# A residual stream kept feature by feature, with the norm's token factor multiplied into the accumulators of the next stage

## The reference

```python
def rmsnorm(x, g):
    return x * rsqrt(mean(x * x, axis=-1) + EPS) * g      # one factor per token, one gain per feature

def hybrid_layer(x, ...):                                  # first block
    h = rmsnorm(x, norm_g)
    aq, ak, av, az, bqk, bv, bi, bf, bo, bz, ga, gb = split(h @ w_in)
    q, k = rope(rmsnorm(heads(aq))), rope(rmsnorm(heads(ak)))
    oa = rmsnorm(diff_attention(q, k, av, lam)) * silu(az)   # 8 heads of 2 x 64, values of 128
    qk = silu(causal_conv(bqk))                              # 8 mLSTM heads
    hb = sigmoid(bo) * rmsnorm(mlstm(qk, bv, bi, bf)) * silu(bz)
    u = sigmoid(ga) * (oa @ w_out_a) + sigmoid(gb) * (hb @ w_out_b)
    return x + u @ w_o

# second block, one layer
h = rmsnorm(x, g_mix)
q_r, k_r, v_r, g_r, q_s, k_s, v_s, gate_a, gate_b = split(h @ w_in_2)
ret = group_norm(retention(rotary(q_r), rotary(k_r), v_r)) * silu(g_r)
sb = stick_breaking(q_s, k_s, v_s)
x = x + (sigmoid(gate_a) * (ret @ p_ret) + sigmoid(gate_b) * (sb @ p_sb)) @ w_out
x = x + square(relu(rmsnorm(x, g_mlp) @ w_up)) @ w_down
# after the last layer
return rmsnorm(x, g_final)
```

## Time and profile before

| | |
|---|---|
| median of three runs | 3214.42 us (3212.61 to 3216.8) |
| the profiled execution | 3216.47 us, span 3214.7 us |
| TensorE busy | 3179.6 us (99%) |
| GpSimd busy | 2072.9 us (64%) |
| VectorE busy | 1391.6 us (43%) |
| ScalarE busy | 843.1 us (26%) |
| moved by DMA | 298.58 MB, 93 GB/s in the mean |
| mean granted clock of TensorE | 0.999 |

### The profile page before, as it was taken

The page is one execution under the profiler, slowest core; times in us unless marked ns, Lnnn a source line. Parts: engine busy times, 40 slices in busy tenths (PEclk is TensorE's granted clock), DMA queues, the critical chain, the costliest instruction groups (busy, mean ns, idle before and its releaser), DMA issues.

```text
span 3214.7 us, 49199 instructions
## 1 busy us (share of the span) xinstructions
PE 3179.6 (99%) x15732; PEld 2676.8 (83%) x15732; DVE 1391.6 (43%) x2224; ACT 843.1 (26%) x1831; POOL 2072.9 (64%) x2052
## 2 busy tenths in 40 slices
PE   7999999999999999999999999999999999999999
PEld 6888888888888888888888888888888888888887
DVE  6777651237776531256663113111366652231121
ACT  5555340025554430032221012011122220021021
POOL 5556657765556567766666776666666657766665
PEclk9999999999999999999999999999999999999999
DMA  3222222232222222322222222223322222222222
GB/s 123 91 88 83 98 82 94 98 103 80 90 85 89 95 85 97 104 94 89 82 88 85 95 101 92 93 98 103 101 85 85 85 72 98 98 96 94 98 98 98
DMA packets 89615, 298.58 MB, mean 93 GB/s; under 512 B 12576, under 2 KB 13472, under 8 KB 89520
## 3 DMA queue, kind: packets, MB, share of 16 engines
q1 hardware_dynamic: 74592, 271.61, 25.3%
q10 hardware_dynamic: 14928, 25.67, 2.6%
HBM read 282.52 MB, written 2.13 MB: 89 GB/s over the span
## 4 chain that ended last, share of the span: by engine, by line
PE 95%; DVE 1%; DMA 1%; ACT 1%; POOL 1%; issue 0%; ACTq 0%; SPq 0%; POOLq 0%; DVEq 0%
PE bank L575 29%; PE bank L577 29%; PE bank L576 29%; PE bank L680 2%; PE bank L741 1%; PE bank L717 1%; PE bank L804 1%; PE bank L730 1%; PE bank L837 1%; POOL w_lo L559 0%; PE bank L786 0%; PE bank L675 0%; PE bank L693 0%; PE bank L821 0%; PE bank L822 0%
## 5 line engine op out<-in xcount | busy, mean ns | idle before, releaser
L559 POOL TENSOR_TENSOR w_lo<-raw,w_hi 128x512 fp32r<-128x512 f32 x1024 | 1385.4, 1353 | 85.4
L556 POOL TENSOR_SCALAR w_hi<-raw 128x512 fp32r<-128x512 f32 x1024 | 704.8, 688 | 1033.9 <-DMA raw<-in_w_in 699.3
L575 PE MATMUL bank<-h_lo,w_hi 128*128 128x512 f32 (+1 forms) x2912 | 1126.6, 387 | 5.9 <-POOL w_lo L559 4.8
L577 PE MATMUL bank<-h_hi,w_hi 128*128 128x512 f32 (+1 forms) x2912 | 1115.2, 383 | 0.0
L576 PE MATMUL bank<-h_hi,w_lo 128*128 128x512 f32 (+1 forms) x2912 | 1114.0, 383 | 0.0
L575 PEld LDWEIGHTS bank<-h_lo,w_hi 128*128 128x128 f32 x2912 | 548.4, 188 | 110.1 <-POOL w_lo L559 6.0
L577 PEld LDWEIGHTS bank<-h_hi,w_hi 128*128 128x128 f32 x2912 | 548.2, 188 | 108.5
L576 PEld LDWEIGHTS bank<-h_hi,w_lo 128*128 128x128 f32 x2912 | 548.8, 188 | 102.7
L1533 DVE TENSOR_TENSOR x<-x,bank 128x512 f32<-128x512 f32 x64 | 44.0, 687 | 391.4 <-PE bank L577 391.1
L575 PE MATMUL bank<-w_lo,up_hi 128*128 128x512 f32 x512 | 199.5, 390 | 0.0
L577 PE MATMUL bank<-w_hi,up_hi 128*128 128x512 f32 x512 | 199.2, 389 | 0.0
(11 more groups left out here) (291 smaller groups left out, 4254.1 us busy)
## 6 DMA issues: line engine op xcount, KB each, us to landing
raw<-in_w_in SPq DMA_DIRECT2D x288, 512.0 KB, 3.3
raw<-in_w_up SPq DMA_DIRECT2D x64, 512.0 KB, 3.3
raw<-in_w_down SPq DMA_DIRECT2D x64, 512.0 KB, 3.3
raw<-in_w_out_a SPq DMA_DIRECT2D x16, 512.0 KB, 3.3
raw<-in_w_out_b SPq DMA_DIRECT2D x16, 512.0 KB, 3.2
raw<-in_w_o SPq DMA_DIRECT2D x16, 512.0 KB, 3.3
raw<-in_p_ret SPq DMA_DIRECT2D x16, 512.0 KB, 3.3
raw<-in_p_sb SPq DMA_DIRECT2D x16, 512.0 KB, 3.2
```

The lines of the kernel that those rows point to most:

```text
L556: nc.gpsimd.tensor_scalar(m.w_hi[:, slot, w], m.raw[:, slot, w], 1.0, 0.0, ALU.mult, ALU.add).then_inc(s["w_step"], 1)
L559: nc.gpsimd.tensor_tensor(m.w_lo[:, slot, w], m.raw[:, slot, w], m.w_hi[:, slot, w].bitcast(F32), ALU.subtract).then_inc(s["split"], 1)
L575: nc.tensor.matmul(dst, hi, rhs_lo, start=first, stop=False, **more)
L577: return nc.tensor.matmul(dst, hi, rhs_hi, start=False, stop=last, **more)
```

## The change

`x` is kept feature-major, eight tiles of 128 features by 512 tokens, like every other activation. The host turns input and output. The projections become ordinary panels: `gemm` with the weights stationary, one bank each, 24 matmuls (48 for the down projection, over two panels). So the transposes, the half-width panels and the held panels go.

The norm's gain is one number a feature, now a column: `h = x * g` is split without waiting for the root. The token factor `r = rsqrt(mean(x^2) + eps)` is the same for all features, so it commutes with the matmul, and is multiplied in afterwards. The squares are summed over the eight tiles in `ssq`; one plain fp32 matmul with a 128 x 128 matrix of ones sums over the partitions and leaves the sum in all of them; two ScalarE operations make `r_b`, 128 x 512. VectorE multiplies the accumulator of a panel in place by `r_b` (`scaled`) before anyone reads it. The readers wait for the semaphore `scaled` in place of `used`. Not multiplied are the retention's queries and keys (there the cosine and sine tables are multiplied by `r_b` once a layer, and so loaded again each layer) and the up panels, where one operation takes max(accumulator, 0) times `r_b`. That makes 272 multiplied accumulators: 80 in a layer of the first block (32 in the head loop and last head, 32 in the pairs, 16 in the merge), 56 in one of the second.

On TensorE, at the start of a stage after a norm:

```diff
-            def first_panels():
...
-                early, late = slice(0, 2 * P), slice(2 * P, S)
-                turn_block(2)
...
-                half(0, early)
-                turn_block(3)
...
-                half(1, early)
...
+            def first_panel():
+
+                gemm(m.h_hi, m.h_lo, "h_ready", at.at("norm", times=KT))
                 at.add("norm")
...
+            def mean_square():
+
+                misc_bank()
+                pe.wait_ge(s["ssq_ready"], at.at("norm"))
+                nc.tensor.matmul(misc[:], m.ones[:], m.ssq[:], start=True, stop=True).then_inc(s["ms_done"], 1)
...
-                first_panels()
+                first_panel()
+                mean_square()
+                h_gemm()
                 pe.wait_ge(s["masks_ready"], 6)
                 group_sum(1, 0)
                 h_gemm()
                 group_sum(0, 0)
+                gate_rows(range(0, 6))
                 value_turns(0)
-                gate_rows()
+                gate_rows(range(6, KT))
```

With `ready`, `gemm` waits ahead of each of the eight tiles for that tile's low part. On ScalarE:

```diff
+            def norm():
+                for n in range(KT):
+                    act.wait_ge(s["x_done"], at.at("norm", times=KT) + (n + 1))
...
+                    activation(m.h_hi[:, n], m.x[:, n], ACT.Copy, scale=m.g_col[:, n:n + 1]).then_inc(s["h_hi_ready"], 1)
+                    if n > 1:
+                        act.wait_ge(s["ssq_added"], at.at("norm", times=KT) + n)
+                    activation((m.sq if n else m.ssq)[:], m.x[:, n], ACT.Square).then_inc(s["xsq_ready"], 1)
                 at.add("norm")
...
+            def root_row():
+                act.wait_ge(s["ms_done"], at.at("norm"))
+                own(activation(m.r_b[:], misc[:], ACT.Ln, bias=m.col[:, 2:3], scale=1.0 / D))
+                act.sem_inc(s["misc_free"], 1)
+                activation(m.r_b[:], m.r_b[:], ACT.Exp, scale=-0.5).then_inc(s["r_ready"], 1)
```

On VectorE, the multiplication, the norm and the head loop:

```diff
+            def scaled(read_here=False):
+
+                c = panel_done()
+                tt(acc[c][:], acc[c][:], m.r_b[:], ALU.mult).then_inc(s["scaled"], at.add("scaled"))
...
+            def residual_add(n, panels):
+                at.add("panel", panels - 1)
+                c = panel_done()
+                own(tt(m.x[:, n], m.x[:, n], acc[c][:], ALU.add))
+                dve.sem_inc(acc_free[c], 1)
+
+            def h_low(n):
+                dve.wait_ge(s["h_hi_ready"], at.at("norm", times=KT) + (n + 1))
+                stt(m.h_lo[:, n], m.x[:, n], m.g_col[:, n:n + 1], m.h_hi[:, n].bitcast(F32), ALU.mult,
+                    ALU.subtract).then_inc(s["h_ready"], 1)
+
+            def add_and_norm(panels):
+                for n in range(KT):
+                    residual_add(n, panels)
+                    dve.sem_inc(s["x_done"], 1)
+                    h_low(n)
+                    dve.wait_ge(s["xsq_ready"], at.at("norm", times=KT) + (n + 1))
+                    if n:
+                        own(tt(m.ssq[:], m.ssq[:], m.sq[:], ALU.add))
+                    dve.sem_inc(s["ssq_added"], 1)
+                dve.sem_inc(s["ssq_ready"], 1)
...
-                with at.loop(A_HEADS - 1, panel=4, acc=4, a=1, own=DVE_A) as i:
+                with at.loop(A_HEADS - 1, panel=4, acc=4, scaled=4, a=1, own=DVE_A) as i:
+                    c = scaled()
                     weights()
-                    cosines(0, 1, 1)
-                    rotate_qk(0, 1, 1)
-                    cosines(1, 1, 2)
+                    cosines(0, 1, 1, c)
+                    c = scaled()
+                    rotated(0, 1)
+                    queries_split()
+                    cosines(1, 1, 2, c)
                     key_squares_low(1)
-                    rotate_qk(1, 1, 2)
-                    take_panel()
+                    rotated(1, 1)
+                    scaled()
+                    keys_split(1, 2)
                     head_normalised()
-                    head_gate()
+                    c = scaled()
                     masked(1, 1)
+                    head_gate(c)
+                    other_maxima(1)
                     head_branch(i)
```

`masked` now takes the first of the four maxima, `other_maxima` the rest. At the end `y = x * g * r_b` is one operation a tile, after `r_b`, and goes out in eight stores of 256 KB:

```diff
+            dve.wait_ge(s["r_ready"], at.at("norm"))
+            for n in range(KT):
+                stt(m.y[:, n], m.x[:, n], m.g_col[:, n:n + 1], m.r_b[:], ALU.mult, ALU.mult).then_inc(s["y_ready"], 1)
```

592 lines of the change are left out of this document (261 added, 331 removed).

## The result

The changed kernel takes 3266.88 us (3265.97 to 3269.1, 4 runs), the kernel before beside it 3213.78 us: ratio 1.0165, 95% interval 1.0147 to 1.0182. It is slower by 53 us, where I forecast 12, with 3249 as the upper end. The profiled execution took 3267.22 us, its span 3265.4.

A forecast was written before the change was run, and what follows sets the result against it. TensorE, busy 3179.6 of 3214.7 us, was taken as the bound. Norms -26, start 0, end +5.5, head loop +18, last heads +10, second block +3, pairs +2: +12.5 on 3214.4 gives 3227, stated as 3226; range 3198 to 3249.

The forecast's parts named there:

- The head loop, +18 for the turns: First block's head loop: late V copy makes TensorE wait, 1.3 us a turn, fourteen turns, +18 us (0 to 36).
- The clock, put at nothing in the sum: TensorE at half clock behind waits: no term in the forecast's sum; 1.4 us lost behind a 1.9 us wait before.
- rival 3: Waits of 2.2 us in the head loop, likewise at last heads, lower the clock: 3247 us; chance 0.15, including slowest multiplication.
- The start, 0: Start to first scores: mean square waits 4 us, first scores about where they were; 0 us (-3 to +3).
- The norms, -26: Five norms between stages: transposes and waits go, 5 us each; scores' waits behind norms give 1 to 2 more; -26.
- The last heads, +10: Last head of a layer: V's multiplication behind gate rows, `o_sb` wait 3.7 us, about +5 a layer, +10 (4 to 14).
- The multiplication, 0.69: VectorE's in-place multiplication of 272 accumulators: 0.69 us each (0.51 to 1.65), covered in merges, up and down panels.
- The pairs of heads, +2: Pairs of heads: only the first of a layer waits; +2 us on the eight pairs (0 to 5).
- The end, +5.5: Kernel's end: 13.7 us from the last add to the span's end, 6.4 before; +5.5 us (4.5 to 7).
- The second block, +3: Second block's turns: key's low part has 0.33 us cover against 0.7 more, 0.4 a turn, 8 turns, +3 us.
- The rule on SBUF's ports: VectorE with at most one SBUF input, outside two-port modes, doesn't contend with GpSimd; with two it does. No sum term.

The follow-up runs named there:

- the second experiment: The changed kernel with ScalarE's logarithm and root of the keys' squares put ahead of V's copy in the head loop: 3245.96 us, ratio 1.0094.
- the kernel that it was made from: The changed kernel with V's multiplication put ahead of the keys' rotation on VectorE in the head loop: 3223.01 us, ratio 1.0027.

## Why the prediction was wrong

The direction was right, and so was the place where most of it is lost; the size was a quarter. The two profiled executions differ by 50.7 us, where the sum had 12.5. Of the 38 us between them 27 are the turns of the head loop (45 for 18), a good half of that the clock; 6.6 are the start. By its own steps:

- **The head loop, +18 for the turns.** This is the step that failed. It had 1.2 us of wait at the value turns. It followed V's multiplication to V's copy, and stopped there: it took the copy as the only thing for which the turns wait. They also wait for the bank that ScalarE's logarithm empties, behind the copy. The copy was 0.95 us late, and the logarithm's 0.25 + 0.69 us behind it make that the 1.95 to 2.0 measured; the second experiment put the logarithm ahead and found 1.2.
- **The clock, put at nothing in the sum.** The prediction left it to rival 3, with a chance of 0.15 and 3247 us; the terms of that rival's sum (31, 14 and 8) don't say which is the clock's. The waits came to 1.95 and the clock to 8 x 1.64 = 13. So rival 3's mechanism is what happened, 20 us above its time: 25.7 of waits at the value turns, 13 of half clock behind them, 6.0 for `o_sb`, 2.7 for the keys' squares, some 3 by which the turns grew beyond their waits (31.80 less 29.63 is 2.17, for a wait of 1.95), and 1.7 of half clock behind the second layer's first scores make up the 51.4 us that the two head loops' rows of the table show. Because the wait had been taken at 1.2, this case got too small a chance.
- **The start, 0.** It failed too: +6.6. The prediction followed the chain to the mean square (4.9 us of wait for the 4 forecast) and `r_b`, and not what stands in VectorE's queue behind the sum of squares: lambdas, a split of the gate weights and conversions, 9.6 us from 26.44 to 36.06, where the same steps had taken 4.9 before, from 26.77. There the first thing behind them was the cosine product at 32.86; now it is the multiplication for which ScalarE, the keys and TensorE wait. The granted clock adds to it: 0.50 from 22.9 to 29.7 and from 40.0 to 46.8, where before it was 1.00 from 18.6 on.
- **The norms, -26.** Right. From the last pair's output turns to the next first scores the difference fell by 4.4, from those of the second layer to the retention's first turn by 4.7, over the two norms of the third layer (between its last turn of retention values and the next layer's first) by 10.5. That is about 5 a norm, as forecast.
- **The last heads, +10.** The number came out by luck. The waits for `o_sb` are 3.0 each as against 3.7. From there to the first turn of `hs` it is 1.7 and 3.1 us longer than before, by the half clock and not by the further wait that the step had: 10.8 in all.
- **The multiplication, 0.69.** 0.697 in 272 rows. The cover in the merges held, twice over. In the up and down panels it held too: 349.6 us from one `ones` product to the next, for 64 panels of 5.45.
- **The pairs of heads, +2.** From the first turn of `hs` to the last, the two layers take 0.9 and 0.7 us more.
- **The end, +5.5.** The tail is 14.1 us for 13.7.
- **The second block, +3.** The key's low part waits 3.5 us in eight, 0.44 each for 0.4. The turns grew by more, 0.6 to 0.9 us each in the six that can be measured from one to the next; what the rest is stays open.
- **The rule on SBUF's ports** (the Trainium skill, SBUF — State Buffer, Who interferes with whom): the trace after agrees. The 272 multiplications, with one SBUF input, took between 0.678 and 0.700 us each, with GpSimd busy 63% of the span; the keys' rotation, with two, took 1.65 from 143.54 on, where GpSimd's `w_lo` ran from 142.96 to 144.64. As forecast, the sum didn't rest on it.

## What to carry to other kernels

When an operation is put ahead of a reader, follow not only the reader but all that stands behind it in the reader's queue, and see which of those steps frees something that the bound engine writes into. Where in a queue a step stands can cost more than the step: here moving one of four multiplications gave back 44 us, and leaving out all 272 where they stood gave back 40. A wait that is put into a sum needs a price for the clock beside it, once it nears the waits behind which the traces show half clock. And before multiplying, ask which consumers normalise anyway: here 32 of the 272 multiplications cancel in the queries' and keys' own norm, and without them the kernel went from 3220.8 to 3205.6 us. An experiment that doubles a step says nothing of stretches in which the step doesn't stand; count its instructions there first.

## What the runs showed of the hardware

- **Waits of about 2 us brought half clock in some cases and not in others.** In the changed kernel, 12 value turns came 1.95 to 2.29 us late, and 8 of them were followed by a stretch at 1.2 GHz that cost 1.64 us. In the kernel that differs by queries and keys not multiplied, 14 came 0.94 to 1.83 late, and behind none did the granted clock fall. That is no sharp limit: with the keys' squares ahead and V's multiplication alone, a wait of 1.85 us was followed by half clock (at 1372), while with the mask conversions moved one of 2.13 was not (at 145). Outside the start, no stretch at half clock in these profiles stands behind a wait shorter than 1.85 us.
- **Small edits changed the spread of times, and the load doesn't explain it.** The kernel before stays within 6 us over 27 runs. With the last head's multiplication moved the kernel took 3213 to 3228 from one execution to the next, and which turns ran over differed between the profiles of such kernels. But the kernel that it was made from, with VectorE just as busy (23.9 of 29.6 us a turn), stays within 4.3 us over 8 runs. So VectorE's load by itself doesn't make the spread, and what does stays open. That the late turns are those whose two-input steps meet GpSimd's instructions is what single rows suggest (1.65 us for 0.69), and was not tried by itself.
